# A streaming encoder layer on one Trainium2 core: the attention projection's dense pieces in quarters of a block at nine places of a tile's weave, in place of halves at five

## The reference

```
h   = RMSNorm_pre(x)
c   = h @ w_in       # columns: recurrence inputs | q, k, v of the attention | two branch gates
A   = RWKV-7 time mixing   # 8 heads of 64, a 64x64 state per head, token after token
Bd  = differential attention  # 4 heads, masked in chunks of 64 tokens
mix = sigmoid(gate_A) * (A @ w_out_a) + sigmoid(gate_B) * (Bd @ w_out_b)
x   = x + RMSNorm_post(mix @ w_o)
x   = x + RMSNorm_post_ffn(SwiGLU(RMSNorm_pre_ffn(x)))
```

## Time and profile before

| | |
|---|---|
| time, median of 3 runs | 1016.3 us (1015.36 to 1016.56) |
| the profiled execution's own time | 1017.05 us |
| its span | 1015.3 us |
| PE busy | 963.6 us, 95% of the span |
| DVE, ACT, POOL busy | 437.9, 285.5, 550.9 us |
| granted TensorE clock, mean over the span | 0.996 |
| chain that ended last | PE 82%, DVE 5%, ACT 4%, POOL 4%, DMA 2% |

### The profile page before, as it was taken

The page is one execution under the profiler, slowest core; times in us unless marked ns, Lnnn a source line. Parts: engine busy times, 40 slices in busy tenths (PEclk is TensorE's granted clock), DMA queues, the critical chain, the costliest instruction groups (busy, mean ns, idle before and its releaser), DMA issues.

```text
span 1015.3 us, 23360 instructions
## 1 busy us (share of the span) xinstructions
PE 963.6 (95%) x9472; PEld 914.6 (90%) x9472; DVE 437.9 (43%) x868; ACT 285.5 (28%) x814; POOL 550.9 (54%) x606
## 2 busy tenths in 40 slices
PE   5999999989998898889999999999999999999996
PEld 5999999967978787778899899999999999999996
DVE  5366478276553546555456463333333333100003
ACT  5213444355554223332213451111111111111111
POOL 6667899623445234143459424555555555665670
PEclk9999999999999999999999999999999999999999
DMA  8332322422232111060126421322233222323232
GB/s 247 90 85 81 84 74 73 128 74 86 78 86 81 35 55 35 34 210 23 28 89 214 125 60 48 99 84 83 83 92 93 83 83 86 92 78 93 79 94 89
DMA packets 138212, 89.65 MB, mean 88 GB/s; under 512 B 5482, under 2 KB 130128, under 8 KB 138128
## 3 DMA queue, kind: packets, MB, share of 16 engines
q1 hardware_dynamic: 129508, 73.04, 25.3%
q10 hardware_dynamic: 8620, 15.42, 4.4%
HBM read 79.26 MB, written 9.19 MB: 87 GB/s over the span
## 4 chain that ended last, share of the span: by engine, by line
PE 82%; DVE 5%; ACT 4%; POOL 4%; DMA 2%; issue 2%; ACTq 1%; DVEq 0%; SPq 0%; POOLq 0%
PE dense L1055 68%; PE side L1135 3%; DMA w_raw<-in_w_o 1%; POOL S L753 1%; POOL w_lo L753 1%; PE side L1178 1%; PE side L1204 1%; PE side L963 1%; PE side L1256 1%; PE side L882 1%; PE side L896 1%; DMA xs<-in_x_prompt 1%; PE side L937 1%; POOL w_hi L748 1%; POOL S L748 1%
## 5 line engine op out<-in xcount | busy, mean ns | idle before, releaser
L748 POOL TENSOR_SCALAR w_hi<-w_raw 128x256 fp32r<-128x256 f32 (+1 forms) x255 | 158.7, 642 | 354.2 <-PE dense L1055 339.8
L753 POOL TENSOR_TENSOR w_lo<-w_raw,w_hi 128x256 fp32r<-128x256 f32 (+1 forms) x255 | 318.4, 1271 | 9.8
L1055 PE MATMUL dense<-h_hi,w_hi 128*128 128x272 f32 (+2 forms) x1376 | 298.4, 295 | 2.6 <-DVE h_lo L1700 1.5
L1055 PE MATMUL dense<-h_hi,w_lo 128*128 128x272 f32 (+2 forms) x1376 | 289.7, 289 | 0.0
L1055 PE MATMUL dense<-h_lo,w_hi 128*128 128x272 f32 (+2 forms) x1376 | 288.9, 289 | 0.0
L1055 PEld LDWEIGHTS dense<-h_hi,w_hi 128*128 128x128 f32 x1376 | 218.5, 189 | 13.1 <-issue 8.4
L1055 PEld LDWEIGHTS dense<-h_lo,w_hi 128*128 128x128 f32 x1376 | 219.0, 190 | 0.0
L1055 PEld LDWEIGHTS dense<-h_hi,w_lo 128*128 128x128 f32 x1376 | 217.6, 190 | 0.0
L1055 PE MATMUL dense<-S,w_hi 128*128 128x272 f32 (+2 forms) x648 | 109.3, 289 | 0.0
L1055 PEld LDWEIGHTS dense<-S,w_hi 128*128 128x128 f32 x648 | 92.1, 188 | 0.2
L1055 PE MATMUL dense<-S,w_lo 128*128 128x272 f32 (+2 forms) x324 | 68.2, 288 | 0.0
(11 more groups left out here) (272 smaller groups left out, 1334.4 us busy)
## 6 DMA issues: line engine op xcount, KB each, us to landing
w_raw<-in_w_ffn_in SPq DMA_DIRECT2D x44, 512.0 KB, 3.7
w_raw<-in_w_in SPq DMA_DIRECT2D x43, 512.0 KB, 3.9
w_raw<-in_w_ffn_out SPq DMA_DIRECT2D x16, 448.0 KB, 3.7
gates<-gst ACTq DMA_DIRECT2D x16, 272.0 KB, 2.1
w_raw<-in_w_ffn_out SPq DMA_DIRECT2D x8, 512.0 KB, 3.7
w_raw<-in_w_o SPq DMA_DIRECT2D x6, 512.0 KB, 5.3
w_raw<-in_w_out_a SPq DMA_DIRECT2D x5, 512.0 KB, 3.6
mb<-gates ACTq DMA_DIRECT2D x1, 2176.0 KB, 9.0
```

The costliest lines, as they stand in the source:

```text
L748: ins = nc.gpsimd.tensor_scalar(hi[:, q], raw[:, q], 1.0, 0.0, ALU.mult, ALU.add)
L753: ins = nc.gpsimd.tensor_tensor(lo[:, q], raw[:, q], hi[:, q].bitcast(F32), ALU.subtract)
L1055: ins = pe.matmul(acc[:, bk, 0:tn], w, r[:, t0:t0 + tn], start=first and n == 0, stop=final and n == 2)
```

## The change

The `outB` blocks are cut in four pieces (1 k-tile, 6 matmuls) in place of two. The weaves of tiles 1 to 3 hold nine pieces in place of five: the four empty turns and the places of f0 to f4 before are all filled. The weave of tile 0 holds seven. The fronts and tile 4 keep their number of places. POOL's one step that is tied to a piece of `outB` 7 is renamed; it was the second of two pieces and is now the second of four.

```diff
-    fill = pieces + [dense("outB", i, p, 2) for i in range(8) for p in range(2)] + [dense("outE", i) for i in OUT_EARLY]
+    fill = pieces + [dense("outB", i, p, 4) for i in range(8) for p in range(4)] + [dense("outE", i) for i in OUT_EARLY]
...
-        fills_, state = [filler(1) for _ in range(5)], state_rows(t)
+        fills_, state = [filler(1) for _ in range(9 if t else 7)], state_rows(t)
         if t:
-            (ymean, yvar, yfin), (f0, f1, f2, f3, f4), (c0, q, ya, c1) = post_rows(t - 1), fills_, state
-            s += weave(invert_rows(t + 1), [c0, ymean, f0, [], yvar, f1, [], q, f2, ya, f3, [], c1, f4, []])
+            (ymean, yvar, yfin), (f0, f1, f2, f3, f4, f5, f6, f7, f8), (c0, q, ya, c1) = post_rows(t - 1), fills_, state
+            s += weave(invert_rows(t + 1), [c0, ymean, f0, f1, yvar, f2, f3, q, f4, ya, f5, f6, c1, f7, f8])
...
-            elif step == ("dense", "outB", 7, 1, 2):
+            elif step == ("dense", "outB", 7, 1, 4):
                 units_up_to(UNIT_OF[("outE", 2)][0][0])
```

## The result

The changed kernel takes 1020.78 us in the median of 19 runs (1019.12 to 1029.27), the kernel before 1017.31 us in 19 runs on the same chip. The ratio is 1.0041, its 95% interval 1.0029 to 1.0054: slower by about 4.2 us (the two medians lie 3.5 us apart). The forecast time was built on the 1016.3 us of three runs of the kernel before, 1.0 us under the median of the 19. The profiled execution took 1019.12 us with a span of 1017.3 us, the one of before 1017.05 and 1015.3 us.

What follows compares the result with a forecast made beforehand. PE was taken as the bound, busy 95% of the span; +1.3 - 2.75 + 0.75 + 0.5 + 1.5 + 0.5 + 1.5 = +3.3 us on 1017.05 gave 1020.35, less 0.75 for the median 1019.6 us, range 1018.4 to 1021.0.

Steps and rivals of the forecast that it cites:

- Interruptions: 13 new places where PE's dense matmuls are broken into, at 0.05 to 0.2 us each: about +1.3 us (0.65 to 2.6).
- Idle time won in the weaves: Tiles 0 to 3: new pieces cover PE's waits for drains, -0.4, -1.2, -0.35 and -0.8 us, in sum -2.75 us.
- Fronts of tiles 2 and 3: Second `sb1` waits for DVE's `rb` beside a piece 0.75 us shorter: +0.75 us in tile 2, +0.5 in tile 3.
- Neither costs PE anything: POOL's split for `outB` 2 and 3 in tile 2's front and the DMA into `mb` were to cost PE nothing.
- `final` of tile 3 to `sk`: Up to tile 4's `sk`, ACT's drains and DMA issues are the bound; two halves beside them become quarters: +1.5 us.
- Rest of tile 4: Seven more places lose 0.75 us of cover each, between nothing and 5.25 us in all: taken as +0.5 us.
- POOL at the end of tile 4: POOL does `yrs` before its last `outE` unit, so PE waits 1.8 us instead of 0.3 at `outE` 4: +1.5 us.
- No change: Rival: tile 4 needs less cover than thought; without its 3.5 us the sum is -0.2 us, 1016.1 us; chance 0.27.
- Faster: Rival: DVE and ACT run ahead, so waits in fronts and behind `yfin` shrink too; 1012.4 us at 10 us hidden; chance 0.15.
- Clock: Rival: waits in tile 4's front and ahead of `outE` 4 halve the clock, +1.5 to 1.6 us for one; chance 0.16.
- if the stretch from `outL` 3 on changes its length: Sign against the forecast: the part of the kernel from `outL` 3 on was to keep its length.

Runs made afterwards that it cites:

- late stores: ACT's four DMA issues for the prompt's last state moved from `final` to a later `yrs`: changed kernel 1019.17 us, kernel before 1017.85 us.
- the pairs: Changed kernel with two quarters of `outB` instead of one behind `final` of tile 3 and `tok` of tile 4: 1016.38 us, again 1016.07 us.
- POOL's order undone: Changed kernel with `outE` 1 moved ahead of tile 4's `yrs` again, so POOL splits its last `outE` unit first: 1019.48 us, ratio 1.0030.
- pairs in the fronts too: The pairs, plus two quarters behind `xi` in the fronts of tiles 2 and 3 and two places fewer in tile 3's weave: 1019.93 us, ratio 1.0002.
- tiles 0 and 1 alone: Kernel before with seven and nine gate pieces in the weaves of tiles 0 and 1, halves of `outB` behind them: 1021.12 us, ratio 1.0035.
- late loads: ACT's four DMA issues loading the sample's state moved into tile 1's weave: kernel before 1017.99 us, changed kernel 1020.86 us, the pairs 1014.98 us.

## Why the prediction came out right, and where not

The forecast was 1019.6 us, in its own range of 1018.4 to 1021.0; measured were 1020.78. Of the 1.2 us between them 1.0 is the starting point, 1016.3 us where 19 runs give 1017.31; forecast was a change of +3.3 us, measured are 4.2 us by the ratio and 3.5 by the medians. By its steps:

- **Interruptions, +1.3 us: wrong, about 0.** PE's busy time over the stretch is the same to 0.1 us, and idle times too short to be listed (under 0.15 us) sum to no more than before. The price came from one pair of gaps with 0.05 us and was raised to 0.1 and 0.2 for other shapes with no row behind it; at 0.05 x 13 it would have been 0.65 us and nearer.
- **Idle time won in the weaves, -2.75 us: right in sum.** Idle time in tiles 0 to 3 fell by 0.9 us although the fronts' two waits grew by 1.9, so about 2.9 went elsewhere: 2.2 in the six groups of the earlier trace rows, and 0.2 as the net of the "issue" holes (1.03 us gone; 0.8 us in two new ones, which the changed order brings every time and no term had). By tiles it was less right: idle time in tiles 0 and 1 fell by 0.7 us, where 1 to 2 us were named as a sign. Tile 0's new wait at L1025 (0.9 us) was foreseen only as "a tanh now delays a drain".
- **Fronts of tiles 2 and 3, +0.75 and +0.5: right in place, too small.** 1.38 - 0.19 = +1.2 us and 1.13 - 0.38 = +0.75 us. In tile 3 the whole piece counts, where a smaller `xi` was thought to spare 0.25. In tile 2, 0.45 us come on top, and the step that failed is another: "Neither costs PE anything", said of POOL's split of the unit for `outB` 2 and 3 behind `xi`. POOL's and DVE's timelines after show DVE's first expansion beside that split at 0.81 us, where the same instruction took 0.42 before, with POOL idle (the second, of 0.43, is in the earlier trace rows):

```profile
416.23 2.97 POOL L753 TENSOR_TENSOR w_lo<-w_raw,w_hi 128x256 fp32r<-128x256 f32 x4
```

```profile
417.81 0.81 DVE L1707 TENSOR_TENSOR gain<-xp,cst 128x256 f32<-128x256 f32 x1
...
418.99 0.49 DVE L1707 TENSOR_TENSOR gain<-xp,cst 128x256 f32<-128x256 f32 x1
419.51 0.49 DVE L1876 TENSOR_TENSOR rb<-side,cst 128x128 f32<-128x128 f32 x2
```

  The two are 0.45 us longer together, and `rb` comes that much later. The Trainium skill (SBUF — State Buffer, Who interferes with whom) has the second input of a VectorE instruction with two inputs in SBUF come through a read port that it shares with GpSimd, and calls this shared pair an exclusive lock. The trace agrees as far as it goes: both inputs of this expansion lie in SBUF, while DVE's other instructions beside the split (a transpose of one input, and `gt` with one input in PSUM) took 0.30 and 0.76 us, before 0.30 and 0.75. The second expansion, which meets only the split's last 0.2 us, took 0.49 instead of 0.43.
- **`final` of tile 3 to `sk`, +1.5: right.** 0.88 + 0.73 - 0.44 = +1.2 us, all on ACT's `ag`. That ACT's chain with its DMA issues sets it is shown by the late stores (0.9 of the 1.6 us go, and 0.5 of the rest is a wait for DVE a step on), that cover decides it by the pairs.
- **Rest of tile 4, +0.5: about 0.1,** the rest of the 2.8 us. The lower bound was nearly right.
- **POOL at the end of tile 4, +1.5: right to 0.1 us.** 1.56 us at `outE` 4. But its cause was put too narrowly: with POOL's order undone the time at full clock stayed, as the first `outL` waited 1.72 us.
- **The rivals.** *No change* falls: tile 4 had no slack. *Faster* falls: the fronts' waits grew. *Clock* is true in part and not as it was told. Its amount, +1.5 to 1.6 us for one fall, was about right: 2.0 ± 0.7 us more lost to the clock over 31 runs. Its places were not: in the profile of the changed kernel the clock is 1.00 from 487.1 to 531.6 us, right behind both of the waits that were named.

The sign "if the stretch from `outL` 3 on changes its length" did come, by -0.8 us, but that stretch varies from profile to profile of unchanged code: from the first `outL` to PE's last matmul it is 482.1 us before, 481.4 and 481.8 in the two profiles of the changed kernel, and 481.3 and 483.0 in the two of the kernel with pairs.

So the sum was +3.3 us, and the change cost 1.9 us in the pair of profiles, 2.4 us in the mean of many at full clock, and 2.0 us through the clock: 4.4 together, where the ratio gives 4.2. The forecast hit the time with one term of 1.3 us too many and one rival's effect of 2 us too few. The mechanism of tile 4 was right; that the total came so near is in part luck, two errors that cancel.

The clock needs a word. One rule of the Trainium skill (Perfetto Trace Analysis, Matmul Optimizations) has the matmul engine's power scale with its use, so that matmuls should run back to back in batches. One comparison agrees: the changed kernel with its waits at tile 4 lost 8.0 us, the one with pairs there 4.7. Three do not. With POOL's order undone the waits are as long (1.72 us for 1.56) and the loss was 5.8 us. With pairs in the fronts too, tile 4's waits are short (0.48 and 0.32 us) and the loss was 7.7. And the kernel with tiles 0 and 1 alone, batches of 12 throughout and 1 us more of waits in all, lost the most, 9.0 us. What stays open is which wait, if any, brings a fall, and so why the change loses 2 us more. The same kernel, the one with pairs, was profiled twice with the same waits ahead of 468 us (0.41 and 0.60 us at L983 in both). The windows show the clock at half for most of one stretch in the first, and full in the second:

```profile
464.00:468.00 4.00, 2.98 (x54) 2.57 (x53) 1.62 (x4) 0.95 (x4) 0.00 (x0) 1.00 0.01 4
468.00:472.00 4.00, 4.00 (x40) 2.96 (x38) 2.40 (x10) 0.84 (x2) 0.00 (x0) 0.64 0.00 0
```

```profile
464.00:468.00 4.00, 2.99 (x69) 2.54 (x68) 2.05 (x8) 0.56 (x3) 0.00 (x0) 1.00 0.02 4
468.00:472.00 4.00, 4.00 (x41) 2.99 (x40) 1.43 (x6) 1.76 (x6) 0.00 (x0) 1.00 0.00 0
```

The first is the run of 1019.25 us, the second that of 1013.61.

## What to carry to other kernels

When filler pieces are cut smaller, look first for the places where one piece was just long enough, most of all where a tile has no work of its own to cover the next engine's queue; leave the pieces there at their old size and cut only the others. Undoing the order that brings a wait does not help if what is short is work: the wait moves to the next reader. A change of a few microseconds should be compared at equal clock too, over many runs, before a cause is looked for in the instructions; and falls of the clock behind the last matmul should not be counted.

## What had not been expected of the hardware

- The granted clock falls at places that differ between executions of one kernel. A fall to 0.50 (1.2 GHz) lasted about 3.4 us, and in six cases in the 14 profiles 6.8 us. One stands at 332 us, behind the 2.52 us of idle time, in 8 of the 11 profiles of kernels without late loads, and in none with; others stood between 395 and 536 us, and in one kernel at 218 and 614 us. Executions of the kernel with pairs, the same code, ranged from 1013.3 to 1019.5 us.
- In all 14 profiles the clock also falls behind PE's last matmul, where it costs nothing.
- Cutting pieces of 12 matmuls into 6, with smaller matmuls of other shapes between, cost PE no busy time that can be seen (185.4 against 185.3 us in stretches of 205.7 and 203.7 us).
- A DVE expansion of 0.42 us took 0.81 us beside POOL's split of a weight unit. `rb`, for which PE waits, came 0.45 us later by this and the next expansion (0.49 for 0.43): POOL delayed PE without PE waiting for POOL.
- PE's idle times for which no engine is named (0.2 to 1.0 us, in the middle of a row of matmuls) stand at the same matmul in traces of one order of the schedule, with other sizes, and at another in another order.
